# Attention's row factors turned through memory instead of by TensorE, and its sums scaled six units later

## What is computed

```
p = masked_softmax(q k^T * scale);  o = p v
nsa: o = g0 * o_cmp + g1 * o_slc + g2 * o_win      # compressed, selected, window; 8 heads of 64
dsa: o = softmax over 256 selected keys            # 8 heads of 64
y_a = o_nsa @ w_branch_nsa ; y_b = o_dsa @ w_branch_dsa
merged = sig(gA) * y_a + sig(gB) * y_b ; h = h + merged @ w_out
```

## Time and profile before

| | |
|---|---|
| median of 3 runs | 1644.32 us (1642.51 to 1646.56) |
| the profiled execution | 1645.87 us |
| its span, first to last instruction | 1643.9 us |
| PE busy | 1584.0 us, 96% |
| DVE busy | 1157.6 us, 70% |
| ACT busy | 650.0 us, 40% |
| POOL busy | 638.0 us, 39% |
| DMA | 171.10 MB, mean 104 GB/s |

### The profile page before, as it was taken

How to read it: one execution, slowest core, us unless ns; L and a number is a source line. 1 busy time by engine, 2 the same in 40 slices (tenths; PEclk the granted TensorE clock), 3 DMA queues, 4 the chain that set the end, 5 groups by cost and what they waited for, 6 DMA issues and landing times.

```text
span 1643.9 us, 24585 instructions
## 1 busy us (share of the span) xinstructions
PE 1584.0 (96%) x9008; PEld 1334.9 (81%) x9008; DVE 1157.6 (70%) x2021; ACT 650.0 (40%) x1269; POOL 638.0 (39%) x442
## 2 busy tenths in 40 slices
PE   6999999999998989999999998999999999999997
PEld 5897888888797878898887786888888888878885
DVE  5744889999545667777665167766667776667978
ACT  5543322121555667767321144322222222344445
POOL 4233664121330144433221215454444444445454
PEclk9999999999999999999999999999999999999999
DMA  6032546331605010010255241333333335474533
GB/s 224 15 92 65 127 113 163 103 103 45 172 29 129 14 52 27 15 40 27 78 166 159 64 162 33 116 109 97 96 97 97 96 97 173 161 262 160 149 114 122
DMA packets 173303, 171.10 MB, mean 104 GB/s; under 512 B 25856, under 2 KB 126208, under 8 KB 173184
## 3 DMA queue, kind: packets, MB, share of 16 engines
q1 hardware_dynamic: 173184, 169.53, 34.1%
HBM read 122.04 MB, written 47.45 MB: 103 GB/s over the span
## 4 chain that ended last, share of the span: by engine, by line
PE 50%; DMA 5%; DVE 2%; issue 1%; SPq 1%; POOL 0%; ACT 0%; DVEq 0%; ACTq 0%
PE psA L1657 9%; PE psA L1659 8%; PE psA L1658 8%; PE psT L1657 5%; PE psT L1658 5%; PE psT L1659 5%; DMA wd<-in_w_down_dram 4%; PE psT L1664 3%; PE psT L1878 3%; PE psA L1767 1%; PE psA L1768 1%; DVE h L2501 0%; DMA scratch_h<-h 0%; DMA s<-scratch_gates 0%; POOL w_lo L447 0%
## 5 line engine op out<-in xcount | busy, mean ns | idle before, releaser
L447 POOL TENSOR_TENSOR w_lo<-w_raw,w_hi 128x1024 fp32r<-128x1024 f32 (+2 forms) x52 | 119.9, 2310 | 266.4 <-ACT w_hi L442 266.1
L1257 POOL TENSOR_TENSOR w_lo<-w_sum,w_hi 128x1024 fp32r<-128x1024 f32 x44 | 115.9, 2635 | 123.4 <-ACT w_hi L1542 123.4
L1479 ACT ACTIVATE s<-s,nmax 128x640 f32<-128x640 f32 (+7 forms) x192 | 144.0, 752 | 30.1 <-DVE nmax L2355 28.6
L1280 POOL TENSOR_TENSOR w_lo<-act_raw,w_hi 128x512 fp32r<-128x512 f32 x77 | 107.8, 1401 | 106.8 <-ACT w_hi L1570 106.8
L1664 PE MATMUL psT<-ident,s 128*128 128x128 f32 x816 | 120.5, 278 | 0.8 <-ACT s L1479 0.8
L442 ACT CAST w_hi<-w_raw 128x1024 fp32r<-128x1024 f32 (+2 forms) x52 | 52.5, 1014 | 148.8 <-PE psA L1659 82.6
L2445 DVE COPY pT<-psT 128x512 f32<-128x512 f32 (+1 forms) x116 | 69.6, 600 | 54.9 <-PE psT L1664 54.7
L1664 PEld LDWEIGHTS psT<-ident,s 128*128 128x128 f32 x816 | 94.3, 141 | 17.2 <-issue 7.5
L2576 DVE TENSOR_TENSOR w_lo<-wd,w_hi 128x512 fp32r<-128x512 f32 x77 | 89.1, 1161 | 24.3 <-ACT w_hi L1577 24.0
L1570 ACT CAST w_hi<-act_raw 128x512 fp32r<-128x512 f32 x77 | 47.9, 622 | 125.8 <-PE psT L1659 58.7
L2245 DVE TENSOR_SCALAR_CACHE_REDUCE equal<-score,bit_try 128x512 f32<-128x512 f32 (+2 forms) x93 | 93.7, 1008 | 0.0
(11 more groups left out here) (380 smaller groups left out, 4696.1 us busy)
## 6 DMA issues: line engine op xcount, KB each, us to landing
act_raw<-scratch_act SPq DMA_DIRECT2D x77, 256.0 KB, 3.0
w_raw<-in_w_in_dram SPq DMA_DIRECT2D x24, 512.0 KB, 4.1
scratch_act<-act SPq DMA_DIRECT2D x33, 256.0 KB, 2.1
scratch_act<-act_sum SPq DMA_DIRECT2D x33, 256.0 KB, 2.1
wd<-in_w_down_dram SPq DMA_DIRECT2D x33, 256.0 KB, 3.0
scratch_gates<-gate_out SPq DMA_DIRECT2D x32, 256.0 KB, 2.9
gates<-scratch_gates SPq DMA_DIRECT2D x30, 256.0 KB, 4.0
a<-in_w_gate_dram SPq DMA_DIRECT2D x22, 256.0 KB, 3.2
```

Of the source, the lines that this page charges most:

```text
L447: nc.gpsimd.tensor_tensor(lo, raw, hi.bitcast(F32), ALU.subtract).then_inc(self.lo_done, 1)
L1257: nc.gpsimd.tensor_tensor(lo2[n % RING][:], block_of(n)[:], hi2[n % RING][:].bitcast(F32), ALU.subtract)\
L1280: nc.gpsimd.tensor_tensor(lo2[slot][:, 0:512], act_raw[n % 6][:], hi2[slot][:, 0:512].bitcast(F32), ALU.subtract)\
L1479: a_.activation(s_sb[v % SR][:, 0:n], s_sb[v % SR][:, 0:n], ACT.Exp, scale=-1.0, bias=nmax[:, BR[a], i, h:h + 1], accum_out=psum_p[:, BR[a ...
```

## The change

- `r_wide`, GpSimd's widening of it, the four transposes a tile and the bank that they took are gone; the group "r" leaves `groups6`, and `tiles6` is built on its own.
- `row_factors` now also multiplies with the branch gate (a second 128 x 8 instruction on VectorE, after a wait for the first) for the 16 nsa tiles.
- SP gets `turn_factors(t)`, 24 times: it waits for the reciprocals, stores the 128 x 8 factors to `scratch["factors"]` transposed, as [8, 128], element by element; waits for `scaled` of tile t - 2; waits until the store has landed; and loads them back in two transfers of 64 partitions each, every row broadcast over the 64 partitions of its head, into `factors[t % 2]` (128 x 512).
- In SP's loop `turn_factors(k - 2)` stands right behind `load_q(k)` for k up to 9; then two stand around each `load_q`; the last four stand behind the loop, two ahead of the waits for the merging's gates, two behind them.
- `scaled` reads the SBUF tile `factors[t % 2]` in place of the PSUM bank, and signals a semaphore of its own.
- `F_LAG` goes from 7 to 13 and `Y_LAG` from 8 to 14: the scaling, the adding and the splitting come six steps later; `STEPS6` grows by six. ScalarE's copy into `acc[t % 2]` still stands at `O_LAG` = 6.

```diff
@@ lags
-    O_LAG, F_LAG, Y_LAG = T_LAG + 1 + V_LAG + 1, T_LAG + 1 + V_LAG + 2, 8
+    O_LAG, F_LAG, Y_LAG = T_LAG + 1 + V_LAG + 1, T_LAG + 1 + V_LAG + 2 + 6, 8 + 6
@@ SP
+        def turn_factors(t):
+            a, i = tiles6[t]
+            sp.wait_ge(rows_done, t + 1)
+            sp.dma_start(rD[t].rearrange("h q -> q h"), psum_r[:, BR[a], i, :], allow_slow_non_contiguous=True)\
+                .then_inc(spilled[t % 2], 16)
+            if t >= 2:
+                sp.wait_ge(scaled_done, t - 1)
+            sp.wait_ge(*factors_spilled(t))
+            for r in range(2):
+                sp.dma_start(factors[t % 2][HD * r:HD * (r + 1)], rD[t:t + 1, r::2, :].to_broadcast([HD, 4, P]))\
+                    .then_inc(spilled[t % 2], 16)
+
         for k in range(2, 2 * NT):
+            if k >= NT + 2:
+                turn_factors(NT + 2 * (k - NT - 2))
             load_q(k)
+            turn_factors(k - 2 if k < NT + 2 else NT + 2 * (k - NT - 2) + 1)
...
+        for t in range(len(tiles6) - 4, len(tiles6) - 2):
+            turn_factors(t)
         sp.wait_ge(t_dve, dve_took["co", NT - 1, 0])
...
         load_gates(1)
+        for t in range(len(tiles6) - 2, len(tiles6)):
+            turn_factors(t)
@@ GpSimd
-            if tile_of(u, R_LAG):
...
-                if a == "dsa":
-                    nc.gpsimd.tensor_copy(r_wide[:], r).then_inc(wide_done, 1)
-                else:
...
-                    nc.gpsimd.tensor_tensor(r_wide[:], r, gate, ALU.mult).then_inc(wide_done, 1)
@@ TensorE
-            if tile_of(u, O_LAG):
-                a, i = tile_of(u, O_LAG)
-                pe.wait_ge(wide_done, t6[a, i] + 1)
-                turn4(group(("r", a, i)), [r_wide[:, 2 * n:2 * n + 2, :].rearrange("p a d -> p (a d)") for n in range(4)])\
-                    .then_inc(t_ps, 1)
@@ VectorE
-            v_.reciprocal(psum_r[:, BR[a], i, :], psum_p[:, BR[a], i, :]).then_inc(rows_done, 1)
+            r = psum_r[:, BR[a], i, :]
+            if a == "dsa":
+                v_.reciprocal(r, psum_p[:, BR[a], i, :]).then_inc(rows_done, 1)
+            else:
+                branch = 1 if a == "slc" else 2
+                then(v_.reciprocal(r, psum_p[:, BR[a], i, :]))
+                v_.tensor_tensor(r, r, nsa_gate[:, i, H * branch:H * (branch + 1)], ALU.mult).then_inc(rows_done, 1)
...
-            factors = psT[:, g6["r", a, i] % 3, :]
-            dve.wait_ge(t_ps, g6["r", a, i] + 1)
+            wide = factors[t % 2][:].rearrange("p n t -> p (n t)")
+            dve.wait_ge(*factors_back(t))
```

More of the change, by code:

```diff
@@ L219, in hybrid_block @@
     psum_r = sb(work, "psum_r", [P, 3, NT, H])
-    sb(work, "skip_merged", [P, HALF + 2 * HALF])
+    factors_even = sb(work, "row_factors_even", [P, 4, P])
+    sb(work, "skip_merged", [P, 2 * HALF])
     c_s = sb(work, "c_s", [P, H, 64])
@@ L610, in hybrid_block @@
     dve_took = nth([k for k in groups6 if not by_act(k)])
-    tiles6 = [k[1:] for k in groups6 if k[0] == "r"]
     t6 = {k: n for n, k in enumerate(tiles6)}
@@ L618, in y_ready @@
         if a == "dsa":
-            eng.wait_ge(t_dve, dve_took["r", a, i])
+            eng.wait_ge(scaled_done, t6[a, i] + 1)
         else:
@@ L650, in hybrid_block @@
     zt_ps, zt_out = sem("zt_ps"), sem("zt_out")
-    spilled = [sem(f"spilled{n}") for n in range(2)]
+    spilled = [sem(f"spilled_or_read_back{n}") for n in range(2)]
     id_ps, relu_done, sc_done = sem("id_ps"), sem("relu"), sem("score_sum")
@@ L698, in hybrid_block, with factors_spilled, factors_back @@
     kD = {"slc": scratch["k_slc"], "win": scratch["k_win"]}
-    gD = scratch["gates"]
+    gD, rD = scratch["gates"], scratch["factors"]
+    factors = [factors_even, factors_odd]
+    def factors_spilled(t):
+        return spilled[t % 2], spill_count(NT + 4 + t % 2) + 48 * (t // 2) + 16
+    def factors_back(t):
+        return spilled[t % 2], spill_count(NT + 4 + t % 2) + 48 * (t // 2 + 1)
     hD, aD = scratch["h"], scratch["act"]
@@ L1193, in _ @@
                 n, r = X_AT.index(u) // 2, X_AT.index(u) % 2
-                lows, wides = sum(1 for v in range(u) if y_of(v - 1)), sum(1 for v in range(u) if tile_of(v, R_LAG))
+                lows = sum(1 for v in range(u) if y_of(v - 1))
                 if lows:
                     pool.wait_ge(yl_done, lows)
-                if wides:
-                    pool.wait_ge(wide_done, wides)
                 windows(nc.gpsimd, n, r, (cx_k, cx_v)[n])
@@ L1235, in _ @@
                 y = y_of_tile("slc", i)
-                pool.wait_ge(t_dve, max(dve_took["r", a, i], dve_took["co", i, 0]))
+                pool.wait_ge(scaled_done, t6[a, i] + 1)
+                pool.wait_ge(t_dve, dve_took["co", i, 0])
                 if n:
@@ L2374, in scaled @@
                     dve.wait_ge(y_done, n)
-                v_.tensor_tensor(yt[:], factors, acc[t % 2][:], ALU.mult).then_inc(t_dve, 1)
+                v_.tensor_tensor(yt[:], wide, acc[t % 2][:], ALU.mult).then_inc(scaled_done, 1)
             elif i < HT:
                 y_free(dve, a, i)
-                v_.tensor_tensor(y_of_tile(a, i)[:], factors, acc[t % 2][:], ALU.mult).then_inc(t_dve, 1)
+                v_.tensor_tensor(y_of_tile(a, i)[:], wide, acc[t % 2][:], ALU.mult).then_inc(scaled_done, 1)
             else:
-                v_.tensor_tensor(y_late("dsa", i), heads(factors, 4), heads(acc[t % 2][:], 4), ALU.mult).then_inc(t_dve, 1)
+                v_.tensor_tensor(y_late("dsa", i), heads(wide, 4), heads(acc[t % 2][:], 4), ALU.mult).then_inc(scaled_done, 1)
         def cmp_out(i):
@@ L2781 @@
         "q_nsa": (nt, P, 8 * P), "q_dsa": (nt, P, 8 * P), "k_slc": (2, 2, HD, seq), "k_win": (2, 2, HD, seq),
-        "gates": (2 * d // P, P, seq), "h": (nt, P, d),
+        "gates": (2 * d // P, P, seq), "factors": (3 * nt, 8, P), "h": (nt, P, d),
         "act": (7, arrays["w_gate"].shape[2] // (2 * P), P, seq // 2)}.items()}
```

18 lines of the change are left out of this document (5 added, 13 removed).

## The result

The changed kernel takes 1690.1 us (median of 4 runs, 1685.0 to 1693.1), the kernel before 1645.4 in the same runs: a ratio of 1.027, with an interval of 1.024 to 1.030, some 44 us slower. The forecast was 1643.7, and no case of it reached so far. The profiled execution of after has a span of 1689.1 us, 45.2 above that of before.

A forecast was written before the change was run, and what follows sets the result against it. TensorE was taken to bound attention. Early tiles +5.4, end +3.5, VectorE +0.7, less 10.2 removed, gave -0.6 us: 1643.7 us on the scale of the medians, with 1639 to 1649 as its own range and 1635 to 1656 overall.

The forecast's parts named there:

- the price of the element store: On SP, each transposed store of 1024 single elements lands in 4.0 us; not below 2.0, no bound above 4.7.
- The slow-store rival: Query loads behind three early stores: each us of landing beyond 4.0 costs three, less 0.9; at 8 us 1654.8; chance 0.22.
- 21 us of room against 8: From reciprocals to later scaling: 21 us on average, against 4 + 1 + 3 = 8 for store, issuing and loads.
- VectorE's waits for factors: Sign of a wrong forecast: VectorE waiting for factors in the long tiles would mean the round trip was misjudged; no size.
- The lower clock: TensorE at clock 0.50 after standing: 1.0 us booked ahead of tile 4, 1.0 at attention's end.
- the early stalls: TensorE waits for late query loads at tiles 3 and 4; tiles 0 to 4 bring +4.9 us, early tiles together +5.4.
- The later steps: At attention's end, tile 23's scaling falls behind dsa's split and starts 2.5 us later; booked as a cost.
- the first rival: Early stalls don't come, as the store lands in 2 us and the queue empties: total -8.5, 1635.8 us; chance 0.28.
- What is removed: In attention, 96 TensorE transposes and waits for GpSimd's widening: 13.2 us in all, 10.2 after tile 7's start.
- The end: After unit 191: dsa's split precedes tile 23's scaling; +2.5 us and 1.0 of lower clock, +3.5 in all.
- Tile 23's factors: At attention's end they add nothing: reciprocals at 788.3 + 8 come before 801.8.
- VectorE beside GpSimd: 24 products reading two SBUF tiles collide with GpSimd: 0.7 us booked, bounds 0 and 5.6; as rival 1648.6 us, chance 0.08.

The follow-up runs named there:

- e8: The changed kernel with factors turned by a single-element load between two stores, division and what follows three units later, compression weights one pass later: 1666.5 us, ratio 1.012.
- e3: The changed kernel with the factors stored straight, 128 pieces of 32 bytes in place of 1024 single elements, output wrong: 1642.2 us, ratio 1.000.
- e7: The kernel before plus five straight stores of factors a tile, each waited for on SP, with no single-element writes: 1664.6 us, ratio 1.013.
- e5: The kernel before plus the 24 single-element stores, with no wait for their landing and no loads back: 1676.0 us, ratio 1.019.
- e1: The changed kernel without stores, loads or waits for factors; tiles of ones instead, so division and gates are left out: 1635.6 us, ratio 0.996.
- e2: The kernel before plus the changed kernel's stores, SP waits and loads of factors into an unread spare tile (last two tiles stored only): 1703.8 us, ratio 1.038.
- e4: e1 with the old lags of 7 and 8 units in place of 13 and 14: 1638.6 us, ratio 0.997.
- e9: e8 with the 4 MB of keys loaded behind tile 7's queries instead of ahead of them: 1665.5 us, ratio 1.012.
- e12: e9 with GpSimd's addition of a tile's sum ahead of the block scores, and division and y transposition one unit earlier: 1657.2 us, ratio 1.009.

## Why the prediction was wrong, point by point

- **The failed step is the price of the element store.** It was taken as 4.0 us, nearest to the transposed loads, with the end above left open; it is 10.1 in the median, from the first tiles to the last. The straight store (1.4 us) takes the ratio from 1.027 to 1.000, so the whole loss hangs on this one transfer. The row was of the same pattern, but of the other direction, and e8 shows that the direction matters. The Trainium skill ("DMA: Bandwidth & Descriptors", Specifications) warned of read-modify-writes below 512 B; the estimate of 8.0 us that I put beside it, a doubling for which the page has no figure, was near, while the 32-byte pieces of e3, also below 512 B, land in 1.4 us.
- **The slow-store rival was the right case, at too low a price.** By its formula 10.1 us give 3 x 6.1 - 0.9 - 0.6 = +16.8. Measured: +44. It had only SP's standing. e7, with some 7 us of standing a tile, shows that part: +21, in the early tiles.
- **What no case had: the store holds other transfers.** Tile 2's queries, issued ahead of it, land in 10.8 us and not 4.7; e5 costs +33 with SP free. This is why the loss goes on in the long tiles (+23.0 at unit 32, +47.4 at the end), where e7 loses nothing and where I had counted 21 us of room against 8. Where the loads of factors are held too, the round trip takes 10 + 1 + 9 us and the room is gone: VectorE's waits for factors, named as a sign of the forecast being wrong, are there.
- **The lower clock was booked too low**, at 1.0 us for the early stalls and 1.0 at the end. Against e1 it costs after 14.2 us: the long stalls bring the clock to 0.50, and TensorE begins again at that level.
- **The parts don't add up exactly.** e7 (+21) and e5 (+33) give 54, and the round trip alone (e2) is +61; with e1's -7 that would be +54 for after, where +44 is measured. The later steps, which e2 hasn't, may account for it; that was not tried.
- **The total of the forecast was near only because its errors cancel.** -0.6 us was the sum for a landing of 4.0 us. At three us of kernel for each of the store it would be some 8 lower for the 1.4 us of e3, as in the first rival (-8.5 at 2 us), and e3 measures -0.3. The early stalls, +6.0 at unit 32 against +4.9, stay though the store is quick, since the queries get nothing back from the queue.
- **What is removed was overrated.** 10.2 us were to come after tile 7. In e1 units 56 to 191 bring 7.1, in e4, with the old steps, 0.9 only. 0.36 us a group of transposes is what the timeline showed, but with the old lags nearly all of it is given back elsewhere; to what, these profiles don't settle. The later steps, booked only as a cost, seem to have given most of the gain, by single executions.
- **The end.** The order came as worked out: dsa's split at 846.67, then the scaling at 850.64. The cost of 3.5 us did not: from the last exponential to the end after takes 859.1 us, e3 858.7, before 861.3. Only e1 against e4 shows 2.4 us. With single profiled executions I can't tell the sign. Tile 23's factors, which were not to add to it, do: VectorE waits 1.48 us for them ahead of that scaling.
- **VectorE beside GpSimd: right, but it hardly came up.** In after 23 of the 24 products run while GpSimd runs nothing, and the other overlaps by 0.13 us; all take 0.67 to 0.69 us, like the faster one of the earlier trace rows. In e3 five overlap, and the four with 0.4 us of overlap or more take 0.95, 1.42, 1.54 and 1.73 us. That is 2.9 us of VectorE, between the 0.7 booked and the bound of 5.6; what it cost the kernel isn't shown. One of the four, GpSimd first:

```profile
...
575.82 1.04 POOL L1233 TENSOR_TENSOR c_s<-c_s,c_st 128x512 f32<-128x512 f32 x1 [17.07 <-DVE c_st L2308]
...
575.87 1.54 DVE L2396 TENSOR_TENSOR y_raw_dsa<-row_factors_odd,acc 128x512 f32<-128x512 f32 x1
...
```

## What to carry to other kernels

Price a transfer by a row of the same direction and the same piece size; a load is no bound for a store, and where no row exists the range must stay open above, with the chances to match. Before a wait goes into a queue that also feeds the bounding engine, list the loads behind it and the loads in flight beside it: both can be held. When steps are moved in a periodic schedule, look at what each engine's stream has at the new place; between e9 and e12 an addition behind 6 us of block scores cost some 14 us of attention. And when a stall is priced, the lower clock behind it belongs to the price (14.2 us here).

## What the runs showed of the hardware that was not expected

- Writing 1024 single elements of 4 bytes from SBUF to memory takes 10.1 us (8.3 to 11.0 where the trace tells it); the same 4 KB in pieces of 32 bytes take 1.4; reading 2048 single elements from memory takes 3.6 to 4.7.
- Little of that time is packets. The store issued at 566.46 has 1042 packets recorded with it, nearly all of them within 1 us from 567.3, and lands at 576.90.
- While such a store is open, other transfers of the same core can land late: query loads 10.8 instead of 4.7 us, a load of factors 9.1 instead of 3.1, weights right behind a store 12 to 14 (e5), though the DMA share is at 0.00 to 0.01 for the last 4 to 5 us of the first two. Not all are held: the query load at 635.82 wasn't, nor tile 7's in e5 (17.1 us, before 17.2). What is waited for the trace doesn't show.
- A load of single elements does nothing of the kind: in e8 the early units come as in e3.
- A store of 4 KB in 8 rows took 16 us to land behind 4 MB of loads issued just ahead of it (e9, e12); e3's straight store, behind these and a load of queries, took 16.7, so the pattern isn't the reason.
